# Modulation's products moved from TensorE to VectorE in the feed-forward parts, and residues placed behind the additions

## The reference, cut to what matters

```python
def swiglu_ffn(h, w_gate, w_up, w_down):                 # first block, both layers
    return (jax.nn.silu(h @ w_gate) * (h @ w_up)) @ w_down
...
mod_x = jax.nn.silu(c) @ w_ada[i] + b_ada[i]             # second block, both layers: 1024 -> 6144
mod_c = jax.nn.silu(c_ctx) @ w_ada[i] + b_ada[i]
...
def sqrelu_mlp(h, w1, w2):                               # second block
    return jnp.square(jax.nn.relu(h @ w1)) @ w2
```

## Time and profile before

| what | us |
|---|---|
| median of 3 runs (lowest, highest) | 2783.05 (2780.53, 2784.03) |
| the profiled execution, its own time | 2781.07 |
| its span | 2779.2 |
| PE busy in the span | 2627.3 (95%) |
| DVE, POOL, ACT busy | 1275.1, 1355.4, 651.1 |
| mean granted clock of PE | 0.975 of full speed |

### The profile page before, as it was taken

The page is one execution under the profiler, slowest core; times in us unless marked ns, Lnnn a source line. Parts: engine busy times, 40 slices in busy tenths (PEclk is TensorE's granted clock), DMA queues, the critical chain, the costliest instruction groups (busy, mean ns, idle before and its releaser), DMA issues.

```text
span 2779.2 us, 38625 instructions
## 1 busy us (share of the span) xinstructions
PE 2627.3 (95%) x14448; PEld 2112.1 (76%) x14448; DVE 1275.1 (46%) x1893; ACT 651.1 (23%) x1222; POOL 1355.4 (49%) x880
## 2 busy tenths in 40 slices
PE   7989999999999989889989999999899999899997
PEld 6667777777777767656768888888788887688886
DVE  6941222253222235445454444444486666555555
ACT  2220000031000013567230000000165553211112
POOL 6365555545555563133536344444343425776661
PEclk9999999999999999999989999999999999999998
DMA  5124444434444441100111111111111111222221
GB/s 188 52 77 159 144 143 145 144 113 139 151 146 148 151 137 54 39 1 1 39 39 61 61 60 60 60 58 59 51 37 40 45 46 36 79 91 98 92 97 53
DMA packets 67372, 235.61 MB, mean 85 GB/s; under 512 B 8144, under 2 KB 9552, under 8 KB 67152
## 3 DMA queue, kind: packets, MB, share of 16 engines
q1 hardware_dynamic: 65792, 233.64, 25.5%
q10 hardware_dynamic: 1488, 0.69, 0.1%
HBM read 232.21 MB, written 2.10 MB: 84 GB/s over the span
## 4 chain that ended last, share of the span: by engine, by line
PE 84%; DVE 8%; issue 3%; ACT 2%; POOL 1%; DMA 1%; DVEq 0%; SPq 0%; ACTq 0%; POOLq 0%
PE ps L650 66%; PE ps L1160 2%; PE ps L1183 2%; PE ps L1048 2%; PE ps L843 2%; PE ps L805 2%; PE ps L1122 1%; PE ps L1034 1%; DVE X L2142 1%; PE ps L769 1%; PE ps L1114 1%; DVE Alo L1734 1%; PE ps L683 1%; DVE tmp L1727 1%; DVE X L1745 1%
## 5 line engine op out<-in xcount | busy, mean ns | idle before, releaser
L501 POOL TENSOR_SCALAR whi<-raw 128x1024 fp32r<-128x1024 f32 x332 | 365.6, 1101 | 1060.3 <-DMA raw<-in_stream 1060.0
L503 POOL TENSOR_TENSOR wlo<-raw,whi 128x1024 fp32r<-128x1024 f32 x332 | 808.9, 2437 | 27.7
L650 PE MATMUL ps<-Ahi,whi 128*128 128x512 f32 (+1 forms) x2128 | 730.7, 375 | 39.9 <-DVE Alo L1734 19.3
L650 PE MATMUL ps<-Alo,whi 128*128 128x512 f32 (+1 forms) x2128 | 720.7, 370 | 0.0
L650 PE MATMUL ps<-Ahi,wlo 128*128 128x512 f32 (+1 forms) x2128 | 719.4, 369 | 0.0
L650 PEld LDWEIGHTS ps<-Ahi,whi 128*128 128x128 f32 x2128 | 376.5, 191 | 131.2 <-issue 21.4
L650 PEld LDWEIGHTS ps<-Ahi,wlo 128*128 128x128 f32 x2128 | 375.7, 190 | 68.9
L650 PEld LDWEIGHTS ps<-Alo,whi 128*128 128x128 f32 x2128 | 376.6, 191 | 66.4 <-issue 0.7
L650 PE MATMUL ps<-hhi,whi 128*128 128x512 f32 x1120 | 373.3, 370 | 19.7 <-DVE X L2142 18.6
L650 PE MATMUL ps<-hhi,wlo 128*128 128x512 f32 x1120 | 373.4, 370 | 0.0
L650 PE MATMUL ps<-hlo,whi 128*128 128x512 f32 x1120 | 370.7, 368 | 0.0
(11 more groups left out here) (291 smaller groups left out, 2782.0 us busy)
## 6 DMA issues: line engine op xcount, KB each, us to landing
raw<-in_stream SPq DMA_DIRECT2D x428, 512.0 KB, 3.8
X<-in_xT SPq DMA_DIRECT2D x2, 1024.0 KB, 6.3
arena<-in_dft SPq DMA_DIRECT2D x1, 2048.0 KB, 16.7
out_xT<-X SPq DMA_DIRECT2D x2, 1024.0 KB, 4.3
X<-in_ctxT SPq DMA_DIRECT2D x1, 1024.0 KB, 19.1
w<-in_stream SPq DMA_DIRECT2D x2, 512.0 KB, 4.3
vec<-in_vec SPq DMA_DIRECT2D x1, 364.5 KB, 7.4
arena<-in_fmap SPq DMA_DIRECT2D x1, 256.0 KB, 12.3
```

Of the source, the lines that this page charges most:

```text
L501: pool.tensor_scalar(whi[:, s, part], raw[:, s, part], 1.0, 1.0, ALU.mult, ALU.mult).then_inc(sem("w_hi"), 1)
L503: pool.tensor_tensor(wlo[:, s, part], raw[:, s, part], whi[:, s, part], ALU.subtract).then_inc(sem("w_split"), 1)
L650: mm = pe.matmul(dst[c], w[:, b % RING, off:off + P], rhs(k, part, c0, n), start=(k == 0 and w is whi and part == 0), stop=(k == kn - 1 an ...
```

## The change

It has three parts.

- In both `swiglu` networks 18 of the 24 `ada` bursts go. DVE takes over: `ada_sums` multiplies the eight row groups of a block (128 x 256 each) by the column of silu(c), and by that of silu(c_ctx), and adds them up in bank 7 of PSUM; the last of the eight goes to SBUF (`tmp`). That is 16 instructions for a block and 32 for a step, put ahead of `hidden` in DVE's step. What is left is a sum over the 128 partitions, which PE makes with a column of ones (`ada_rows`: four float32 matmuls 32 x 128). The burst then stands behind its half of `up`, not in front. The first pair and the last two still go through `ada`. The pairs are grouped 1, 3, 3, 3, 2, so there are five turns and not four; the three in the loop read one bank (`ada_columns`) and stand inside `down`, behind job 1.
- Because the bursts stand behind their half, the blocks are loaded in another order (`FF_ORDER`): gate, ada, up, ada, down, where it was ada, gate, ada, up, down. POOL splits the first, third and fifth.
- In `swiglu` and in `mlp` DVE's residues `hidden_lo` stand behind all eight additions, and in `mlp` the squares `hidden` too.

The diff's core:

```diff
-            return (at - 4) % 5 in (0, 2)
+            return (at - 4) % 5 in (1, 3)
...
+FF_ORDER = (1, 0, 3, 2, 4)
...
+            def ada_rows(name, e, turn, pairs):
+                pe.wait_ge(*when(f"{name}_acc", ADA_SUMS * pairs + ADA_SUMS // 2 * (e + 1)))
+                for c in range(2):
+                    for src in range(2):
+                        at = ADA_GROUP * (2 * c + src)
+                        mm = pe.matmul(ps[at:at + ADA_GROUP, 6, e * P:(e + 1) * P], one_row[:, 2 - turn:2 - turn + ADA_GROUP],
+                                       tmp[:, 2 * e + src, T + c * P:T + (c + 1) * P], start=(turn == 0 and e == 0),
+                                       stop=(turn == ADA_SHARED - 1), skip_group_check=True)
+                mm.then_inc(sem("w_used"), 2)
...
                 with pe.Fori(0, FF_IT // 3) as p:
                     for s in range(3):
-                        step(3 * p + s, B0 + 4 + 5 * s, s, p + 1, FF_SPLITS * p, 5 * p)
+                        i, at = 3 * p + s, B0 + 4 + 5 * s
+                        for part in range(2):
+                            up(i + 1, at, FF_SPLITS * p, part)
+                            if s == 0 and part == 0:
+                                pe.wait_ge(*when(f"{name}_ada", p + 1))
+                            ada_rows(name, part, s, i)
+                        down(i, at + 4, s, FF_SPLITS * p, p + 3 if s == ADA_SHARED - 1 else None)
...
+                def ada_sums(p, pairs, e, at, after_block):
+                    done = ADA_SUMS * pairs + ADA_SUMS // 2 * e
+                    for k in range(KT):
+                        if k % 4 == 0:
+                            dve.wait_ge(*when(f"raw{at % RING}{k // 4}", 80 * p + (16 * (at // RING) + 16)))
+                        if k == KT - 1:
+                            dve.wait_ge(*block_used(15 * p + (at - 5)))
+                        for src in range(2):
+                            acc = ps[:, 7, src * 256:(src + 1) * 256]
+                            row = raw[:, at % RING, k * 256:(k + 1) * 256]
+                            c = csil[:, k, 2 * ADA_SHARED - 2 + src:2 * ADA_SHARED - 1 + src]
+                            if k == 0:
+                                if after_block:
+                                    dve.wait_ge(*when(f"{name}_acc", done + (src - 1)))
+                                mm = dve.tensor_scalar(acc, row, c, None, ALU.mult)
+                            else:
+                                dve.wait_ge(*when(f"{name}_acc", done + (2 * k - 2 + src + 1)))
+                                to = acc if k < KT - 1 else tmp[:, 2 * e + src, T:TT]
+                                mm = dve.scalar_tensor_tensor(out=to, in0=row, scalar=c, in1=acc, op0=ALU.mult, op1=ALU.add)
+                            mm.then_inc(sem(f"{name}_acc"), 1)
...
                     for j in range(2):
-                        hidden(i + 1, b + 3, j)
-                    if slot == ADA_SHARED - 1:
-                        mods(turn)
+                        hidden(i + 1, b + 2, j)
                     for m in range(KT):
                         add_down(i, b + 4, m)
-                        if m < 2:
-                            hidden_lo(i + 1, slot, m)
+                        if m == 3 and shared_columns is not None:
+                            mods(shared_columns + 1, 3 * shared_columns + 1, ADA_SHARED)
+                    for j in range(2):
+                        hidden_lo(i + 1, slot, j)
...
                         for m in range(KT):
-                            if m < 2:
-                                hidden(i + 1, m)
                             add_down(i, 6 * p + (B0 + 2 + 2 * s), m)
-                            if 1 <= m < 3:
-                                hidden_lo(i + 1, (s + 1) % 3, m - 1)
+                        for j in range(2):
+                            hidden(i + 1, j)
+                        for j in range(2):
+                            hidden_lo(i + 1, (s + 1) % 3, j)
```

More of the change, by code:

```diff
@@ L832, in _, with ada @@
             wout(range(8), 6, KT)
-            def ada(at, e, turn, rounds=0):
+            def ada(at, e, turn, turns):
                 first = 2 * (ADA_SHARED - 1 - turn)
                 for half in range(2):
-                    pe.wait_ge(*when(f"raw{at % RING}{half}", 16 * rounds + (16 * (at // RING) + 16)))
+                    pe.wait_ge(*when(f"raw{at % RING}{half}", 16 * (at // RING) + 16))
                     for g in range(4):
@@ L844, in ada, with ada_select @@
                                        raw[:, at % RING, k * 256:(k + 1) * 256], start=(turn == 0 and half == 0),
-                                       stop=(turn == ADA_SHARED - 1 and half == 1),
+                                       stop=(turn == turns - 1 and half == 1),
                                        skip_group_check=True)
                     mm.then_inc(sem("w_used"), 1)
-            def ada_select(name, turns):
-                pe.wait_ge(*when(f"{name}_arow", 2 * turns))
+            def ada_select(name, copies):
+                pe.wait_ge(*when(f"{name}_arow", copies))
                 n = 2 * ADA_SHARED
@@ L869, in swiglu, with up, down @@
                 B0 = B_FF[f]
-                def up(i, at, more, rounds, turn, turns):
-                    for part in range(2):
-                        ada(at + 2 * part, part, turn, rounds)
-                        pe.wait_ge(*when(f"{name}_silu" if part == 0 else f"{name}_mul", 2 * i))
-                        columns(f"{name}_up", [(more + SPLITS[at + 2 * part + 1], at + 2 * part + 1)], X_ONLY,
-                                banks[2 * part:2 * part + 2])
-                    if turn == ADA_SHARED - 1:
-                        ada_select(name, turns)
-                def down(i, at, slot, more):
+                def up(i, at, more, part):
+                    pe.wait_ge(*when(f"{name}_silu" if part == 0 else f"{name}_mul", 2 * i))
+                    columns(f"{name}_up", [(more + SPLITS[at + 2 * part], at + 2 * part)], X_ONLY,
+                            banks[2 * part:2 * part + 2])
+                def down(i, at, slot, more, copies=None):
                     pe.wait_ge(*when(f"{name}_h", 2 * i + 2))
@@ L885, in down @@
                         down_job(name, i, more + SPLITS[at], at, m, h_rhs(slot), X_ONLY, 2)
+                        if m == 1 and copies is not None:
+                            ada_columns(name, copies)
                 for e in range(2):
-                    ada(B0 + e, e, 0)
+                    ada(B0 + e, e, 0, 1)
                 columns(f"{name}_up", [(SPLITS[b], b) for b in (B0 + 2, B0 + 3)], X_ONLY, banks[0:4], ready)
-                def step(i, at, s, turns, more=0, rounds=0):
-                    turn = (s + 1) % ADA_SHARED
-                    if turn == 0:
-                        pe.wait_ge(*when(f"{name}_ada", turns))
-                    up(i + 1, at, more, rounds, turn, turns)
-                    down(i, at + 4, s, more)
+                ada_select(name, 2)
                 with pe.Fori(0, FF_IT // 3) as p:
                     for s in range(3):
-                        step(3 * p + s, B0 + 4 + 5 * s, s, p + 1, FF_SPLITS * p, 5 * p)
-                for i in range(FF_IT // 3 * 3, FF_IT - 1):
-                    step(i, B0 + 4 + 5 * i, i % 3, i // 3 + 1)
+                        i, at = 3 * p + s, B0 + 4 + 5 * s
[5 more added lines that the diff above has]
+                        down(i, at + 4, s, FF_SPLITS * p, p + 3 if s == ADA_SHARED - 1 else None)
+                i = FF_IT - 2
+                at = B0 + 4 + 5 * i
+                for part in range(2):
+                    up(i + 1, at, 0, part)
+                    if part == 0:
+                        pe.wait_ge(*when(f"{name}_ada", 4))
+                    ada(at + 1 + 2 * part, part, 0, 2)
+                down(i, at + 4, i % 3, 0)
                 i = FF_IT - 1
@@ L911, in _ @@
             pe.wait_ge(*when("csil", 2))
+            pe.wait_ge(*when("one_row", 2))
             pe.wait_ge(*when("sel", 1))
@@ L1431, in step @@
                         copy(hhi[:, slot, j, 0:T], tmp[:, j, 0:T]).then_inc(sem(f"{name}_hi"), 1)
+                rows(B0, 1)
                 step(0, B0, 0, True)
```

112 lines of the change are left out of this document (75 added, 37 removed).

## The result

| | median us (lowest to highest, runs) | ratio to before (95%) |
|---|---|---|
| before | 2782.08 (2780.53 to 2784.03, 4) | |
| after | 2747.93 (2744.65 to 2749.90, 4) | 0.9881 (0.9869 to 0.9893) |
| forecast | 2752.5 (2744 to 2774) | |

What follows compares the result with a forecast made beforehand. PE, busy 95% of the span, was taken to bound the kernel. The terms -23.0 + 1.8 - 18.6 + 6.0 + 1.7 + 3.5 = -28.6 us against 2781.07 gave 2752.5 us, range 2744 to 2774.

Steps and rivals of the forecast that it cites:

- The bursts: PE's `ada` bursts in both `swiglu` networks: 0.64 us saved for each of 36, -23.0 us.
- the two more turns: Turns of rows into columns, five per network instead of four: 0.9 us each, +1.8 us.
- The products' margin: First block's 16 products on DVE, 0.40 us apart, end 0.8 us before PE asks in `swiglu`: cost 0.
- The rule of the Trainium skill: Next DVE operation starts after the pipe empties: 16 products take 7.6 us, PE waits 5 us in all, time 2758.
- The rival of products in a chain: Products on DVE wait one for another, 0.585 us apart: PE waits 38 us, time 2790; chance 0.10.
- The waits of `ml0`: PE's waits for DVE's late additions, 17.6 us in `ml0` and 1.0 in `ml1`, go: -18.6 us.
- The tails: Last `down` of `ml0` and `ml1` waits for residues: +6.0 us (5.1 to 8.5) and +3.5, plus +1.7 for the clock.
- The clock: Clock falls behind PE's stand in `ml0`'s tail, +1.7 us; in `ml1`'s, 0 to 1.7 more if it falls.
- the tails of the two `swiglu`: Ends of the `swiglu` loops: over 3 us of PE work covers the last addition and two residues, cost nothing.

Runs made afterwards that it cites:

- after_copy: The changed kernel run once more, unchanged: 2748.72 us, ratio to before 0.9889.
- tails_unrolled: The changed kernel with the last `mlp` step in the old order and VectorE's `swiglu` loop written out as straight code: 2732.66 us, ratio to before 0.9824.
- chained: The changed kernel, but each product on DVE waits for the one directly before it, not the one before that: 2767.26 us, ratio to before 0.9953.
- ff_old: The changed kernel with only `swiglu`'s residues back behind the first and second addition: 2770.43 us, ratio to before 0.9962.
- tails_pad_ff0: The changed kernel with the last `mlp` step in the old order and 165 unused semaphore increments ahead of `ff0`'s loop: 2739.82 us, ratio to before 0.9852.

## Why the prediction was right, and where it wasn't

**The bursts: right.** 0.64 us each was forecast and measured. With the two more turns the sum has -21.2, 10.6 for each network; `ff0` gave 11.3 in after and 12.1 in the same kernel's second trace (`after_copy`), and `ff1` 8.3 in after and 11.4 where DVE didn't stand (`tails_unrolled`). What is short in after is the stands of `ff1`, the one wait behind the products that the prediction didn't have.

**The products' margin: right.** Forecast: 0.40 us apart, the block's end 10.0 us behind the start of the last addition, and 0.8 us to spare; measured: 0.39, 9.1 to 9.9, and 0.8 to 1.65. The estimate was at the narrow end, since outside the stands the products start 2.7 to 3.6 us behind the addition, and not always 3.5. It also counted 18 steps at risk, and there are 16. It was the step with the least certainty, and `chained` shows how narrow it is: at 0.525 the change keeps only 13 of its 33 us. The rule of the Trainium skill that was weighed against it (VectorE: DVE Perf Modes, "The DRAIN you can't avoid") doesn't hold here as it was read: products 0.48 us long start 0.39 apart. The page itself adds that "a next op that is not held starts earlier", and that is the case here. The rival of products in a chain didn't occur. Its price was too high too, since a waiting product starts 0.04 us, not 0.11, behind the other's end.

**The waits of `ml0`: right mechanism, size too small.** The term said -18.6 with `ml1`'s; measured are -22.2 and -1.8. A wait as listed is shorter than what it costs: around one in before, two matmuls start 1.45 us apart where 0.12 is normal, 1.33 us, while the row lists 1.1 a time.

**The tails: right mechanism, one size off.** Sum: 6.0 + 1.7 + 3.5 = 11.2; measured: 7.5 + 6.5 = 14.0. The wait in `ml0` was 4.9, just under the range of 5.1 to 8.5, since DVE got in ahead of POOL; in `ml1` it was 3.5 as forecast. The clock was mis-sized: beyond their waits the tails cost 2.6 and 3.0 us in after, and the sum had 1.7 for the one and 0 for the other (with up to 1.7 beside it). In `after_copy` and `ff_old` `ml1`'s tail costs 5.1, which is 1.6 for the clock: such a price can double from one execution to the next.

**`swiglu`'s residues: wrong, though it didn't show.** The prediction said that the tails of the two `swiglu` cost nothing, which was right, and its sum has no term for the move of their residues. That move is worth 22 us by the medians (19 by the traces) in the new load order and nothing in the old. The two halves of the change give some 8 and 4 us alone (ratios 0.9970 and 0.9985) and 33 together. The prediction moved the splits only as far as they delay the products, and never asked what the kernel would do with the residues left where they were. As the whole change was forecast, the error cancelled.

**The total.** -28.6 forecast, -31.9 between the profiled executions, -33 by the ratio: 5.4 more from `ml0` and `ml1`, 1.6 less from `swiglu` and 2.8 more cost in the tails make -29.6, the sum of the stretches above; what is left is within the spread of single executions. That the total came out 3 to 5 us from the forecast is in part luck, since these misses have different signs.

Not tried: bursts left on PE with the new load order alone, so that what this order costs without the products isn't shown, and other lengths of padding, which would place the edge of the code's blocks.

## What to carry to other kernels

- A reordering that only lets another pass can be worth nothing alone. When blocks are loaded in another order, look at where the engine that prepares them now works, and which instructions with two SBUF inputs run beside it.
- When work is moved behind the end of a loop's step, the last step has nothing to hide it under: write that one out in the old order (10 us here), and count the clock's half speed behind the stand with the stand (1.6 to 3.0 us here behind one of 3.5).
- If an engine stands at a loop's branch back and waits for nothing, shift its code by some instructions before changing the loop; here 60 empty ones took both stands away, and 3 us of `ff1` with them. The loop written out did the same.

## What the runs showed that I had not expected

**Code has a place.** DVE stood 2.6 us (5.1 with the residues moved up) at the two turns of `ff1`'s loop, and at none of `ff0`'s, whose body is of the same make. With 60 instructions ahead of it the stands went; with 165 ahead of `ff0` they were 3.1 and 3.0 us there. The Trainium skill, Runtime: NRT & Kernel Launch, section "Instruction fetch mechanics", describes such a thing: code is fetched in blocks of 256 instructions, of which two are held, and a taken branch outside them waits. The runs agree in that the place decides and the body's length doesn't; with the rest of the block arithmetic they agree in part only, since small stands stayed in `ff1` in `tails_pad_ff0`.

The DMA view shows the reads themselves, and it is this that ties the stands to code. Over the same 230 us of `ff1` (750 to 980), after has:

```profile
q14 instruction: 11, 0.09, 0.1%
```

Two of these reads fall between the last addition and the first product at each turn with a stand. The queue has none at all over 220 us of `ff0`'s loop (325 to 545), nor in `ff1` from 748 to 980 with the 60 increments. With the 165 increments it has 11 in `ff0`'s stretch as well, with two at each of the turns that stand for 3.1 and 3.0 us, and one at each of those that stand for 1.6 and 1.2. The loop written out has 3 in each of the stretches, with no stand: code that is read once, in a straight line, cost no time here, and code read again behind a branch did. Each read is 8 KB, where the section gives 16 KiB for its blocks of 256 instructions; whether that is why the arithmetic fails for the small stands isn't shown.

**Who comes first pays less.** Where DVE's residue was ahead, it took its usual 0.7 or 0.95 us and POOL's instruction was drawn out, as in `ml0`'s tail (1.78 us and not 1.05). Where POOL's subtraction was ahead, it was the residue, which took 1.4 to 3.15 us in after. The kernel before has the same two instructions in both orders. Once the residue is 0.01 us ahead (DVE, then POOL); the other order is that of the earlier trace rows, with 3.06 and 2.39 us:

```profile
1477.50 0.94 DVE L2132 TENSOR_TENSOR hlo<-tmp,hhi 128x768 fp32r<-128x768 f32 x1
1477.51 3.19 POOL L503 TENSOR_TENSOR wlo<-raw,whi 128x1024 fp32r<-128x1024 f32 x1
```

Which of the two engines pays so depends on a tenth of a microsecond in the order of two starts, and here it matters, since additions stand behind DVE's residue and PE waits for them.
